# The lead's expert pairs moved to PSUM banks 0 and 1, and the token transposes moved behind the third pair

## The reference

```python
def peer_ffn(hn, wq, sub_keys, u, v):
    q = (hn @ wq).reshape(bsz, seq, 8, 2, 128)
    sc = einsum("bshpc,hpnc->bshpn", q, sub_keys)      # 16 lists of 128 scores per token
    v1, i1 = top_k(sc[..., 0, :], 16); v2, i2 = top_k(sc[..., 1, :], 16)
    cand = (v1[..., :, None] + v2[..., None, :])       # 256 candidates per head
    top, ci = top_k(cand, 16)
    idx = i1[ci // 16] * 128 + i2[ci % 16]             # 8 x 16 = 128 experts of 16384 per token
    g = softmax(top)
    a = einsum("td,ted->te", x, u[idx])
    return einsum("te,ted->td", g * gelu(a), v[idx])
```

## Time and profile before

| | |
|---|---|
| three runs, us | 4128.77, 4131.63, 4135.46 (median 4131.63) |
| profiled execution, us | 4127.37 |
| its span, us | 4125.3 |
| mean granted clock of TensorE | 0.984 |
| busy: TensorE / VectorE / ScalarE / GpSimd, us | 3961.5 / 2855.0 / 1747.9 / 1163.6 |
| layer 1's lead, us from the span's start | 872.4 to 990.1 |
| layer 2's lead | 2915.7 to 3033.4 |

### The profile page before, as it was taken

The page is one execution under the profiler, slowest core; times in us unless marked ns, Lnnn a source line. Parts: engine busy times, 40 slices in busy tenths (PEclk is TensorE's granted clock), DMA queues, the critical chain, the costliest instruction groups (busy, mean ns, idle before and its releaser), DMA issues.

```text
span 4125.3 us, 59238 instructions
## 1 busy us (share of the span) xinstructions
PE 3961.5 (96%) x19746; PEld 3398.2 (82%) x19746; DVE 2855.0 (69%) x4378; ACT 1747.9 (42%) x3160; POOL 1163.6 (28%) x786
## 2 busy tenths in 40 slices
PE   7999999989999999999999999999799999999998
PEld 5677887779999988888766778877799999888886
DVE  2584341699988977877737833417998889677786
ACT  3533123224666653343335321322256666443343
POOL 1014573311211432222200155642011224222231
PEclk9999999989999999999999999999999999999999
DMA  3112331227878999999721122312378789999995
GB/s 125 49 62 84 104 113 62 92 91 248 297 260 295 389 375 342 357 355 351 257 67 52 57 97 102 118 62 82 135 249 293 268 298 406 365 345 347 340 354 186
DMA packets 360974, 879.45 MB, mean 213 GB/s; under 512 B 27856, under 2 KB 191952, under 8 KB 353872
## 3 DMA queue, kind: packets, MB, share of 16 engines
q1 hardware_dynamic: 153360, 508.20, 34.3%
q0 software_dynamic: 73728, 268.47, 17.3%
q10 hardware_dynamic: 133696, 100.67, 8.1%
HBM read 774.47 MB, written 102.76 MB: 213 GB/s over the span
## 4 chain that ended last, share of the span: by engine, by line
PE 73%; DVE 12%; DMA 4%; DVEq 4%; issue 3%; ACT 2%; ACTq 1%; POOL 0%; SPq 0%; POOLq 0%
PE ps L1202 41%; PE ps L1497 22%; PE ps L1474 3%; DMA raw<-in_experts 2%; DVE wlo L796 2%; DMA act_e<-early_gelu 1%; PE ps L1210 1%; PE ps L1250 1%; DVEq L821 1%; DVE ubuf L1064 1%; DVE acc L1071 1%; DVEq L985 1%; PE ps L1268 1%; PE ps L1261 1%; PE ps L1260 1%
## 5 line engine op out<-in xcount | busy, mean ns | idle before, releaser
L1202 PE MATMUL ps<-xhi,whi 128*128 128x384 f32 (+1 forms) x3328 | 1224.3, 368 | 92.7 <-DVE xlo L817 30.9
L1202 PE MATMUL ps<-xhi,wlo 128*128 128x384 f32 (+1 forms) x3328 | 1192.9, 358 | 0.0
L1202 PE MATMUL ps<-xlo,whi 128*128 128x384 f32 (+1 forms) x3328 | 1192.7, 358 | 0.0
L465 ACT ACTIVATE whi<-raw 128x1024 fp32r<-128x1024 f32 x666 | 698.3, 1054 | 346.3 <-PE ps L1497 254.0
L1202 PEld LDWEIGHTS ps<-xhi,whi 128*128 128x128 f32 x3328 | 632.3, 190 | 168.7 <-issue 79.7
L796 DVE TENSOR_TENSOR wlo<-raw,whi 128x1024 fp32r<-128x1024 f32 x512 | 622.2, 1219 | 141.6 <-ACT whi L465 137.6
L1202 PEld LDWEIGHTS ps<-xlo,whi 128*128 128x128 f32 x3328 | 632.8, 190 | 52.3 <-issue 5.3
L1202 PEld LDWEIGHTS ps<-xhi,wlo 128*128 128x128 f32 x3328 | 631.7, 190 | 52.6
L1497 PE MATMUL ps<-whi,eh 128*128 128x512 f32 x1536 | 601.1, 391 | 23.9 <-DVE el L1163 23.9
L425 POOL DMA_INDIRECT ubuf<-in_up_rows,gidx x256 | 290.0, 1133 | 1124.9 <-DVE small L1064 906.2
L1497 PE MATMUL ps<-wlo,eh 128*128 128x512 f32 x1536 | 599.7, 390 | 0.0
(11 more groups left out here) (206 smaller groups left out, 4813.9 us busy)
## 6 DMA issues: line engine op xcount, KB each, us to landing
raw<-in_experts SPq DMA_DIRECT2D x512, 512.0 KB, 6.4
raw<-in_back SPq DMA_DIRECT2D x112, 512.0 KB, 3.2
gate_table<-gbuf SPq DMA_DIRECT2D x48, 1024.0 KB, 8.8
act_e<-early_gelu ACTq DMA_DIRECT2D x128, 384.0 KB, 7.0
gtile<-gate_table ACTq DMA_DIRECT2D x30, 1536.0 KB, 23.3
raw<-in_front SPq DMA_DIRECT2D x64, 512.0 KB, 3.2
raw<-in_gates SPq DMA_DIRECT2D x48, 512.0 KB, 3.2
early_gelu<-weighted SPq DMA_DIRECT2D x128, 192.0 KB, 5.5
```

Source lines behind the costliest of these rows:

```text
L465: A(whi[:, SLOT[s]:SLOT[s] + 1024], raw[:, SLOT[s]:SLOT[s] + 1024], ACT.Copy).then_inc(rounded[s], 1)
L1202: ins = MM(out, w[:, a:a + P], x[:, c, t0:], start=(i == 0 and n == 0), stop=(i == len(chunks) - 1 and n == 2))
```

## The change

In the lead, pair `i` writes banks 0 and 1; in the blocks, banks 4 and 5 as before. The transposes of the gathered tokens move from ahead of pair 0 to behind pair 2 (`TURN_PAIR`) and go to banks 2, 3 (high) and 6, 7 (low); ScalarE's copy moves behind its Gelus of pair 2, and VectorE's addition reads banks 6 and 7. The first pair now waits for all list copies, the transposes for all scores' use, `turn(1)` for the new `xtok_ready`, and the first block for both Gelus of pair 11. The lead's pairs are written out on TensorE, where five turns of a loop were.

```diff
--- before.py
+++ after.py
@@ -232,6 +232,12 @@
 
         base_col = small[:, 60:61]
 
+        TURN_PAIR = 2
+
+        def up_bank(i, m):
+
+            return m if i < LEAD else 4 + m
+
         GATE_BANK0 = (0, 4, 5)
         BRANCH_BANK0 = (3, 1, 2)
 
@@ -289,7 +295,7 @@
         gt_loaded = [sem(f"gt_loaded{k}") for k in range(2)]
         act_loaded = [sem(f"act_loaded{k}") for k in range(2)]
 
-        xt_turned, xtok_hi, gidx_ready = sem("xt_turned"), sem("xtok_hi"), sem("gidx_ready")
+        xt_turned, xtok_hi, xtok_ready, gidx_ready = sem("xt_turned"), sem("xtok_hi"), sem("xtok_ready"), sem("gidx_ready")
         u_loaded = [sem(f"u_loaded{k}") for k in range(GB)]
         v_loaded = [sem(f"v_loaded{k}") for k in range(GB)]
         dot_done, coef_ready, axpy_done = sem("dot_done"), sem("coef_ready"), sem("axpy_done")
@@ -664,9 +670,6 @@
                     A(pqT[:, l % 2, :], ps[:, l % 4, :], ACT.Copy).then_inc(pq_copied, 1)
                     round_panel(l % 4, L, base + 8 + l // 4 + 1)
 
-                act.wait_ge(xt_turned, L * 2 + 1)
-                A(xtok, ps[:, 0:2, :].rearrange("p a (b n) -> p (a b) n", n=GT), ACT.Copy).then_inc(xtok_hi, 1)
-
                 def early_pair(i, sels=()):
                     for m in range(2):
                         if m:
@@ -675,7 +678,7 @@
                         n = 2 * i + m
                         panel(n % 4, L, FIRST + n // 4)
                         act.wait_ge(early_stored[n % 4], (L * (EARLY // 2) + i // 2) * 16)
-                        A(early(i, m), ps[:, 4 + m, 0:DT], ACT.Gelu).then_inc(early_ready[m], 1)
+                        A(early(i, m), ps[:, up_bank(i, m), 0:DT], ACT.Gelu).then_inc(early_ready[m], 1)
                         round_panel(n % 4, L, FIRST + n // 4 + 1)
 
                 def pick_weights(t):
@@ -710,6 +713,9 @@
 
                 for i in range(LEAD):
                     early_pair(i)
+                    if i == TURN_PAIR:
+                        act.wait_ge(xt_turned, L * 2 + 1)
+                        A(xtok, ps[:, 2:4, :].rearrange("p a (b n) -> p (a b) n", n=GT), ACT.Copy).then_inc(xtok_hi, 1)
                     if i == 2 or i == LEAD - 3:
                         pick_weights(int(i > 2))
                     if i == LEAD - 2:
@@ -1084,7 +1090,7 @@
                         TS(base_col, base_col, float(NK * NK), None, ALU.add)
                         dve.wait_ge(xtok_hi, L + 1)
                         dve.wait_ge(xt_turned, L * 2 + 2)
-                        TT(xtok, xtok, ps[:, 2:4, :].rearrange("p a (b n) -> p (a b) n", n=GT), ALU.add)
+                        TT(xtok, xtok, ps[:, 6:8, :].rearrange("p a (b n) -> p (a b) n", n=GT), ALU.add).then_inc(xtok_ready, 1)
                         V.memset(acc, 0.0)
                     if (t, k) == (1, HALVES - 1):
                         drain()
@@ -1435,16 +1441,11 @@
                     score(l - 1)
                 score(LISTS - 1)
 
-                for n, x in enumerate((xhi, xlo)):
-                    for c in range(KC):
-                        ins = TR(ps[:, 2 * n + c // 4, (c % 4) * P:(c % 4 + 1) * P], x[:, c, 0:GT].bitcast(F32), cst("ident"))
-                    ins.then_inc(xt_turned, 1)
-
-                def early_pair(i, parity, use):
+                def early_pair(i, parity, use, lead=False):
 
                     for m in range(2):
                         pe.wait_ge(early_ready[m], L * EARLY + i)
-                        linear(2 * parity + m, L, FIRST + use, ps[:, 4 + m, 0:DT], xhi, xlo, t0=GT)
+                        linear(2 * parity + m, L, FIRST + use, ps[:, m if lead else 4 + m, 0:DT], xhi, xlo, t0=GT)
 
                 def turn(t):
 
@@ -1453,14 +1454,22 @@
                         ins = TR(ps[:, 6, q * P:(q + 1) * P], eidx[:, q, :], cst("ident"))
                     ins.then_inc(selT_done, 1)
 
-                pe.wait_ge(score_used, L * (LISTS * TB) + (LISTS - 2) * TB)
+                pe.wait_ge(pq_copied, (L + 1) * LISTS)
+                for i in range(TURN_PAIR + 1):
+                    early_pair(L * 0 + i, i % 2, L * 0 + i // 2, lead=True)
+                pe.wait_ge(score_used, (L + 1) * (LISTS * TB))
+                for n, x in enumerate((xhi, xlo)):
+                    for c in range(KC):
+                        ins = TR(ps[:, 2 + 4 * n + c // 4, (c % 4) * P:(c % 4 + 1) * P], x[:, c, 0:GT].bitcast(F32), cst("ident"))
+                    ins.then_inc(xt_turned, 1)
+                for i in range(TURN_PAIR + 1, LEAD):
+                    if i == LEAD - 1:
+                        pe.wait_ge(xtok_ready, L + 1)
+                        turn(1)
+                    early_pair(L * 0 + i, i % 2, L * 0 + i // 2, lead=True)
+                for m in range(2):
+                    pe.wait_ge(early_ready[m], L * EARLY + LEAD)
                 pe.nop(nofuse=True)
-                with pe.Fori(0, LEAD // 2 - 1) as i:
-                    for k in range(2):
-                        early_pair(i * 2 + k, k, i)
-                early_pair(LEAD - 2, 0, LEAD // 2 - 1)
-                turn(1)
-                early_pair(LEAD - 1, 1, LEAD // 2 - 1)
 
                 for b in range(DB):
                     at = LEAD + b * BLOCK
```

## The result

The changed kernel was timed three times, each time beside the kernel before on the same chip:

| | changed, us | before, us | ratio | 95% interval |
|---|---|---|---|---|
| first | 4136.93 (20 runs) | 4130.21 (20) | 1.0015 | 1.0009 to 1.0022 |
| second | 4132.06 (12) | 4130.94 (23) | 1.0002 | 0.9992 to 1.0012 |
| third | 4133.10 (12) | 4128.66 (17) | 1.0009 | 1.0000 to 1.0017 |

What follows compares the result with a forecast made beforehand. VectorE's program was taken to set the lead's pace up to the turn, TensorE's matmuls after it. Terms 2 x (0 + 0 + 0.69 + 0.54) = 2.5 us on 4131.63 gave 4134.1 us, range 4128 to 4141.

Steps and rivals of the forecast that it cites:

- The removed wait: Lead's first matmul: starts 4.2 us earlier without the `max_index` wait, but later panels still await VectorE; worth 0.
- end wait: Behind the lead, before pair 12: waiting for both Gelus costs 0.69 us plus 0.54 loop entry, 1.23 per layer.
- The transposes are covered: Behind pair 2: about 1.8 us of transposes fit the 2.28 us gap before panel 8; layer 2 about 0.65 late.
- The cover behind: Idle time before panel 14 (1.77 us) and the turn (0.67), 2.4 us together, absorbs late transposes.
- Rival (a): Lead at half clock, TensorE late to the turn: slower, bound 4145 us; decides if pair 2 ends 2.9 later; chance 0.04.
- ScalarE's copy has margin: Copy of `xtok` behind pair 2 ends about 911.5, VectorE needs it at 916.11: margin 4.6 us.
- The full clock behind the gap: After the new 1.05 us idle near 990: full clock expected; half-clock stretches would add at most 3.6 us.
- The unrolling costs nothing: Lead's five loop turns as straight code: code loading is the price, taken as 0.
- The sum: Whole kernel, two layers: 2 x 1.23 = 2.5 us slower, median 4134.1 us, +0.06%; chance as worked out 0.80.
- Rival (b): TensorE bounds the lead, so its earlier start carries through: 4126 us, or 4110 with all 12 won; chance 0.03.
- Rival (c): Behind the lead: Gelu wait and loop entry hide in TensorE's queue, costing nothing: 4131.6 us; chance 0.08.
- (d): Code loading stalls the straight lead during gathers: +2 to +8 us, 4136 to 4142; chance 0.05 including half clock at 990.

Runs made afterwards that it cites:

- the last experiments: Low-part subtractions moved from VectorE to GpSimd: kernel before, 8 panels 0.9979, 12 panels 0.9985; changed kernel without end wait, 8, 12, 16 panels: 0.9957, 0.9961, 0.9973.

## Why the prediction was right, step by step

- **The removed wait is worth nothing.** Right. 4.25 us earlier at the first matmul, and at the turn nothing that comes from it, in four profiles (three of the changed kernel and one without the end wait); the variant without the end wait is at 0.9998.
- **The transposes are covered.** Right in the result, off in the row that it was worked out from. I left 0.5 us of the gap before panel 8 in layer 1; in fact TensorE was 0.4 us late there (64.0 against 63.5), and between 0 and 0.5 in the eight layers of the four profiles. The 2.28 us gap that I took for layer 1 was the exception: the other seven leads built as before have 1.15 to 1.64 us there, as their pair 2 takes 10.7 to 11.2 us and not 10.0. The estimate for layer 2 (0.65 us late, from the gap of 1.15) came nearer for both. The cover behind took it all: the turn is late only where panel 14 ran at half clock, which happened without the change too. Rival (a) is not at work. One of my grounds against it was misread, though: I said that both orders pause 3.9 us before pair 2, and it is 5.5 in layer 2 of the kernel before and in both layers of the changed one. Of the 2.9 us at which (a) would decide, that leaves 1.8, for the old order as for the new.
- **ScalarE's copy has margin.** Right: 3.7 us, 4.6 forecast, and the missing 0.9 is the longer pair 2 ahead of the copy. The run with the transposes behind pair 3 overran it by 4.8 us and paid 4.8 per layer.
- **The end wait costs 1.23 us a layer.** Right: from the turn to pair 12 it is 1.13 to 1.19 us more in every profile with this wait. The two terms were 0.69 for the Gelu and 0.54 for the loop entry; measured, the Gelu's end to the next matmul is 0.50 (991.89 to 992.39). The full clock behind the gap was as forecast (1.00).
- **The unrolling costs nothing.** Right, by its own run.
- **The sum.** The rows give 2.4 to 2.7 us, the forecast 2.5, the three timings 1.1, 4.4 and 6.7 us by their medians. In the first timing the forecast of 1.0006 lies just under the interval, so that the first ratio alone would say a larger cost. The profile of that timing doesn't show the missing part where the change is: of its 16 us more than the profile of before, 2.6 are in the lead, and the largest single piece, 6.5 us more on TensorE's wait for `el`, is in the down projection, whose length from first to last matmul lay between 523.9 and 534.8 us in the profiles of kernels that are all alike there. So the mechanism is shown by the rows, by the end wait run alone and by the rest of the change run without it, while the size of the whole is known only to some 2 us. Whether part of the change's cost lies outside the lead stays open.
- **Rival (b)**, that TensorE bounds the lead, fell. What revived the early start was a different edit, as the last experiments showed. **Rival (c)**, a hidden wait, fell by the gap of 1.03 us in every profile with the wait, and **(d)**, code loading, by the unrolled lead run alone.

## What to carry to other kernels

A 12 us wait with one engine's name on it is worth only what the next wait on the same engine leaves: look whether the same releaser stands behind it again, and if every gap of a stretch names one engine, shorten that engine's list. An ordering wait added at a seam between two stages costs what pipelining had hidden there, here the last Gelu plus the entry into a loop, 1.2 us; giving the last item of the stage the next stage's banks avoids it. And an edit that frees an engine too early for its neighbour can be kept without cost until the neighbour is made faster: the two together gave 0.4%, the second alone 0.2%, with eight `low` on GpSimd.

## What was not expected of the hardware

Some of VectorE's operations lasted until GpSimd's subtraction ended (the `cand` addition of 0.43 us grew to 1.56, beside a GpSimd operation of 2.39). The Trainium skill (SBUF — State Buffer, "Terms", the row "shared port pair") says that the pair is locked exclusively for a whole instruction and that the loser blocks fully; the rows agree. The same `tensor_scalar` on `uint32` picks (L1010) was held as well, 1.31 us at 897.65 against 0.18 at 909.30. So a subtraction of 1.2 us moved to GpSimd can cost VectorE more than it takes off, depending on what it falls beside: four more of them in the kernel before, 12 for 8, took 4.8 us off VectorE's list, lengthened its other operations by some 5.5 to 6.2 us more, and the turn came 0.7 and 1.4 us later. The two times, 0.9985 and 0.9979, can't tell them apart.
